# Output projection by Strassen's scheme over all sixteen row tiles, and a changed order in the last attention pair

## The reference

```python
SEQ, D_MODEL = 1024, 2048
def hybrid_layer(x, ..., w_out):
    proj = jnp.einsum('bsd,de->bse', rms_norm(x, norm_g), w_in)
    ...
    mixed = jnp.concatenate([out_a * silu(az), out_b * silu(bz), out_c * silu(cz)], axis=-1)
    return x + jnp.einsum('bse,ed->bsd', mixed, w_out)
```

## Time and profile before

| | |
|---|---|
| timed runs, median of 3 | 2040.82 us (2039.97 to 2043.32) |
| profiled execution | 2044.43 us |
| its span, first to last instruction | 2042.7 us |
| TensorE busy | 2008.2 us, 98% |
| VectorE, ScalarE, GpSimd busy | 1121.9, 891.1, 503.1 us |
| plain second column group, first matmul | 1785.5 us |
| Strassen part, first matmul | 1872.6 us |
| Strassen part, last matmul | 2037.3 us |

### The profile page before, as it was taken

The page is one execution under the profiler, slowest core; times in us unless marked ns, Lnnn a source line. Parts: engine busy times, 40 slices in busy tenths (PEclk is TensorE's granted clock), DMA queues, the critical chain, the costliest instruction groups (busy, mean ns, idle before and its releaser), DMA issues.

```text
span 2042.7 us, 28729 instructions
## 1 busy us (share of the span) xinstructions
PE 2008.2 (98%) x10024; PEld 1690.6 (83%) x10024; DVE 1121.9 (55%) x1733; ACT 891.1 (44%) x1504; POOL 503.1 (25%) x400
## 2 busy tenths in 40 slices
PE   6999999999999999999999999999999999999998
PEld 5788888888888888888888888888888887788787
DVE  7611456465445555555555555555555657613797
ACT  7311343444454445445454445445444556411242
POOL 0000343251531212222221212222122210002565
PEclk9999999999999999999999999999999999999999
DMA  7322424324332222222222222323232274466646
GB/s 236 81 72 71 116 68 109 100 82 103 94 98 78 61 85 78 87 67 72 87 72 85 64 89 79 107 58 98 83 97 71 85 249 145 134 200 222 237 155 196
DMA packets 204559, 223.20 MB, mean 109 GB/s; under 512 B 17336, under 2 KB 143336, under 8 KB 203328
## 3 DMA queue, kind: packets, MB, share of 16 engines
...
...
## 4 chain that ended last, share of the span: by engine, by line
PE 85%; DVE 7%; ACT 2%; DMA 2%; issue 2%; POOL 1%; SPq 0%; DVEq 0%; ACTq 0%; POOLq 0%
PE acc L2266 19%; PE acc L2268 19%; PE acc L2267 19%; PE pv L2504 4%; PE turned L2489 4%; PE scores L2481 2%; PE scores L2478 2%; DVE w_lo L1724 1%; DVE act_lo L2209 1%; DMA w_raw<-in_w_in_dram 1%; PE acc L2616 1%; DVE fast_out L2222 1%; PE acc L2553 1%; PE acc L2555 1%; PE acc L2554 1%
## 5 line engine op out<-in xcount | busy, mean ns | idle before, releaser
L2266 PE MATMUL acc<-act_hi,w_hi 128*128 128x512 f32 x1848 | 737.1, 399 | 2.5 <-DVE w_lo L1724 1.9
L2268 PE MATMUL acc<-act_hi,w_lo 128*128 128x512 f32 x1848 | 722.0, 391 | 0.0
L2267 PE MATMUL acc<-act_lo,w_hi 128*128 128x512 f32 x1848 | 720.7, 390 | 0.0
L2268 PEld LDWEIGHTS acc<-act_hi,w_lo 128*128 128x128 f32 x1848 | 346.9, 188 | 75.4
L2266 PEld LDWEIGHTS acc<-act_hi,w_hi 128*128 128x128 f32 x1848 | 347.5, 188 | 69.5 <-DVE w_lo L1724 4.8
L2267 PEld LDWEIGHTS acc<-act_lo,w_hi 128*128 128x128 f32 x1848 | 347.7, 188 | 65.2
L1724 DVE TENSOR_TENSOR w_lo<-w_raw,w_hi 128x512 fp32r<-128x512 f32 x223 | 199.4, 894 | 358.6 <-ACT w_hi L1239 358.3
L1545 ACT ACTIVATE prob<-prob,neg_max 128x128 f32<-128x128 f32 (+7 forms) x160 | 124.0, 775 | 251.1 <-DVE neg_max L2035 251.1
L1159 POOL TENSOR_TENSOR vz<-raw 32x512 f32<-32x512 f32 x72 | 85.6, 1189 | 468.3 <-ACT sq L1492 465.6
L1239 ACT ACTIVATE w_hi<-w_raw 128x512 fp32r<-128x512 f32 x223 | 139.1, 624 | 137.2 <-PE acc L2268 110.1
L2051 DVE TENSOR_TENSOR pt_lo<-turned,pt_hi 128x1024 fp32r<-128x1024 f32 (+1 forms) x120 | 114.9, 957 | 146.9 <-ACT pt_hi L1553 146.3
...
## 6 DMA issues: line engine op xcount, KB each, us to landing
...
```

The costliest lines, as they stand in the source:

```text
L2266: pe.matmul(acc, hi, xh, start=first, stop=False)
L2267: pe.matmul(acc, hi, xl, start=False, stop=False)
L2268: mm = pe.matmul(acc, lo, xh, start=False, stop=end)
```

## The change

The halves of row tiles now have eight tiles each, tile 8 and tile 9 among them, so that the only left run is the one item of the first column group, which stands first. There are 57 items. For this the last two rows of `mixed` are stored to DRAM, from where halves are loaded again. The products stand in another order, with other blocks. Products 2 and 6 (`FAST_ON_TOP`) start without clearing their banks and add onto what products 0 and 4 left there, after these were merged into one block; the sum goes into the other block. That saves merges: 40 and the 8 of the left run in place of 72. A run's merges are spread over 6 steps (`MERGE_STEPS`). The row sums stand at other steps, eight for each of five products. The buffers of the three output column groups change roles.

In the last pair VectorE does the sums of rounds 0 and 1 in front of the weight split that is due there, and at slot 28 (`LATE_FIRST`) the scale in front of a split.

```diff
@@ -112,31 +112,33 @@
...
 MIX_BUFS = 4
+LATE_FIRST = 28
 
...
 FAST_CGS = (2, 3)
-FAST_ROWS = (list(range(7)), [7] + list(range(LAST + 1, KT)))
-FAST_LEFT = (LAST - 1, LAST)
+FAST_ROWS = (list(range(LAST - 1)), [LAST - 1] + list(range(LAST + 1, KT)) + [LAST])
 FAST_K = len(FAST_ROWS[0])
-FAST_WEIGHTS = (((0, 1), ALU.subtract, (1, 1)), ((1, 0), ALU.subtract, (0, 0)), ((0, 0), ALU.add, (1, 1)),
-                ((0, 0), None, None), ((1, 1), None, None), ((0, 0), ALU.add, (0, 1)), ((1, 0), ALU.add, (1, 1)))
-FAST_ROW_SUMS = (None, None, ((0, 0), ALU.add, (1, 1)), ((1, 0), ALU.add, (1, 1)), ((0, 0), ALU.add, (0, 1)),
-                 ((1, 0), ALU.subtract, (0, 0)), ((0, 1), ALU.subtract, (1, 1)))
-FAST_INTO = (((1, 0, ALU.add), (1, 1, ALU.add)), ((0, 1, ALU.add), (0, 0, ALU.add)),
-             ((0, 0, ALU.add), (1, 1, ALU.add)), ((0, 1, ALU.add), (1, 1, ALU.subtract)),
-             ((1, 0, ALU.add), (0, 0, ALU.subtract)), ((1, 1, ALU.add),), ((0, 0, ALU.add),))
-FAST_RUNS = [("product", 0), ("product", 1), ("left", 0), ("left", 1), ("left", 2)] + [("product", q) for q in range(2, 7)]
-LEFT_ROWS = (FAST_LEFT, FAST_LEFT, FAST_LEFT[1:])
-LEFT_COLS = (FAST_CGS[0] * HALF, FAST_CGS[1] * HALF, 0)
+FAST_WEIGHTS = (((0, 1), ALU.subtract, (1, 1)), ((1, 0), ALU.subtract, (0, 0)), ((0, 0), ALU.add, (0, 1)),
+                ((0, 0), None, None), ((0, 0), ALU.add, (1, 1)), ((1, 1), None, None), ((1, 0), ALU.add, (1, 1)))
+FAST_ROW_SUMS = (None, None, ((1, 0), ALU.subtract, (0, 0)), ((1, 0), ALU.add, (1, 1)), ((0, 0), ALU.add, (1, 1)),
+                 ((0, 0), ALU.add, (0, 1)), ((0, 1), ALU.subtract, (1, 1)))
+FAST_ON_TOP = (2, 6)
+FAST_INTO = (((1, 0, ALU.add),), ((0, 1, ALU.add), (0, 0, ALU.add)), ((1, 1, ALU.add),),
+             ((0, 1, ALU.add), (1, 1, ALU.subtract)), ((1, 1, ALU.add),), ((1, 0, ALU.add), (0, 0, ALU.subtract)),
+             ((0, 0, ALU.add),))
+FAST_RUNS = [("left", 2)] + [("product", q) for q in range(7)]
+LEFT_ROWS = {2: (LAST,)}
+LEFT_COLS = {2: 0}
 RUN_SIZE = [FAST_K if kind == "product" else len(LEFT_ROWS[q]) for kind, q in FAST_RUNS]
...
 FAST_SLOTS = 4
+MERGE_STEPS = 6
 SPLIT_BEFORE = Q_OUT + EARLY + KT
...
 FAST_SUMS = (len(FAST_INTO) - 2) * FAST_K
-ROW_SUM_STEP = [first + j for first in (9, 16, 23, 30, 37) for j in range(FAST_K)]
+ROW_SUM_STEP = [first + j for first in (4, 12, 20, 28, 36) for j in range(FAST_K)]
 MERGES = []
@@ -241,7 +243,7 @@
...
         elif e < n:
-            out += own[2 * (n - e - 1):2 * (n - e)]
+            out += [own[i] for i in range(len(own)) if e + 1 + i * MERGE_STEPS // len(own) == n]
     return out
@@ -549,7 +551,7 @@
...
         t_los = [t_lo0[:], t_lo1[:], w_lo[:, 0, :], w_lo[:, 1, :]]
-        merged_into = [fast_out[0], fast_out[1], res]
+        merged_into = [res, fast_out[1], fast_out[0]]
 
@@ -931,8 +933,11 @@
...
                 load_early_rows(n)
+                if n == 7:
+                    store_pair(LAST - 1)
                 if n == 10:
                     sp.wait_ge(mix_lo, mixed_by(KK_GATED, 1))
+                    sp.wait_ge(mixed_saved, 16 * LAST)
                     load_gate(LAST, last_column)
@@ -959,20 +964,27 @@
...
 
-            def load_fast_residual(c, t):
-                cols = slice(FAST_CGS[c] * HALF, (FAST_CGS[c] + 1) * HALF)
-                sp.dma_start(fast_out[c][:, t, :], x_rows[t * P:(t + 1) * P, cols]).then_inc(x_in[c], 16)
+            def load_fast_residual(t):
+                cols = slice(FAST_CGS[1] * HALF, (FAST_CGS[1] + 1) * HALF)
+                sp.dma_start(fast_out[1][:, t, :], x_rows[t * P:(t + 1) * P, cols]).then_inc(x_in[1], 16)
 
             def load_partial(t):
+                sp.dma_start(fast_out[0][:, t, :], partial[t * P:(t + 1) * P, :]).then_inc(x_in[0], 16)
+
+            def load_first_residual(t):
+                cols = slice(FAST_CGS[0] * HALF, (FAST_CGS[0] + 1) * HALF)
                 sp.wait_ge(out_saved[t], 32)
-                sp.dma_start(res[:, t, :], partial[t * P:(t + 1) * P, :]).then_inc(res_in[t], 16)
+                sp.dma_start(res[:, t, :], x_rows[t * P:(t + 1) * P, cols]).then_inc(res_in[t], 16)
 
...
                 k = FAST_ROWS[kh][j]
-                sp.wait_ge(quarter_done, 3 * (GROUPS + AHEAD) + EARLY - len(ROUNDS) + OUT_ORDER.index(k) + 1)
+                if k == LAST:
+                    sp.wait_ge(out_ready, 2 * NT)
+                else:
+                    sp.wait_ge(quarter_done, 3 * (GROUPS + AHEAD) + EARLY - len(ROUNDS) + OUT_ORDER.index(k) + 1)
                 sp.dma_start(raw_rows(th, kh, j), mixed[k * P:(k + 1) * P, th * HALF:(th + 1) * HALF])\
-                    .then_inc(mix_in[0 if th == kh else 1 + kh], 16)
+                    .then_inc(mix_in[2 * kh + (th != kh)], 16)
 
@@ -999,7 +1011,10 @@
...
                 load_out_quarter(1, kk)
+            sp.wait_ge(o_done, LAST + 3)
+            sp.dma_start(mixed[LAST * P:(LAST + 1) * P, :], vz[:]).then_inc(mixed_saved, 16)
             sp.wait_ge(mix_lo, MIX_ALL)
+            sp.wait_ge(mixed_saved, 16 * PAIRS)
             load_res(1)
@@ -1013,37 +1028,40 @@
...
                         for t in range(2 * (kk - 8), 2 * (kk - 8) + 2):
-                            load_fast_residual(1, t)
+                            load_fast_residual(t)
                 else:
-                    load_rows_again(1, 1, kk - 12)
+                    if kk == 12:
+                        load_rows_again(0, 0, FAST_K - 1)
+                    load_rows_again(1, 0, kk - 12)
                     for t in range(2 * (kk - 12), 2 * (kk - 12) + 2):
-                        load_fast_residual(0, t)
+                        load_partial(t)
             load_terms(2)
-            load_rows_again(1, 1, 4)
+            load_rows_again(1, 0, 4)
             load_terms(3)
-            load_rows_again(1, 1, 5)
+            load_rows_again(1, 0, 5)
             load_terms(4)
             load_terms(5)
-            load_rows_again(1, 1, 6)
+            load_rows_again(1, 0, 6)
             load_terms(6)
             load_terms(7)
+            load_rows_again(1, 0, 7)
             for n in range(8, FAST_ITEMS):
...
                 if 8 <= n < 8 + FAST_K:
-                    load_rows_again(1, 0, n - 8)
+                    load_rows_again(1, 1, n - 8)
                 if 14 <= n < 18:
                     for t in range(2 * (n - 14), 2 * (n - 14) + 2):
-                        load_partial(t)
+                        load_first_residual(t)
                 if 18 <= n < 18 + FAST_K:
                     load_rows_again(0, 1, n - 18)
-                if 28 <= n < 32:
-                    for t in range(2 * (n - 28), 2 * (n - 28) + 2):
+                if 20 <= n < 24:
+                    for t in range(2 * (n - 20), 2 * (n - 20) + 2):
                         save_merged(2, t)
-                if 45 <= n < 49:
-                    save_merged(0, 4 + n - 45)
+                if 48 <= n < 52:
+                    save_merged(0, 4 + n - 48)
             for t in range(4):
@@ -1209,9 +1227,12 @@
...
                 if u == 0:
-                    pool.wait_ge(mix_in[0], mix_landed(0) + 16 * 2 * FAST_K)
-                elif j == 0 and q in (3, 4):
-                    pool.wait_ge(mix_in[q - 2], mix_landed(q - 2) + 16 * FAST_K)
+                    pool.wait_ge(mix_in[0], mix_landed(0) + 16 * FAST_K)
+                    pool.wait_ge(mix_in[1], mix_landed(1) + 16 * FAST_K)
+                elif j == 0 and q == 3:
+                    pool.wait_ge(mix_in[2], mix_landed(2) + 16 * FAST_K)
+                elif j == 0 and q == 5:
+                    pool.wait_ge(mix_in[3], mix_landed(3) + 16 * FAST_K)
                 if u >= 4:
@@ -2132,14 +2153,18 @@
...
                 for slot in range(8, SLOTS + 1):
-                    for n in early_at(slot):
-                        if n % (KT - 1) == 0 and n > 0:
-                            early_sums(n // (KT - 1) - 1)
                     steps(slot)
+                    if slot == LATE_FIRST:
+                        late(slot)
                     for n in early_at(slot)[:1]:
+                        if n % (KT - 1) == KT - 2 and n < EARLY - 1:
+                            early_sums(n // (KT - 1))
                         split_next(n + EARLY_AHEAD)
-                    late(slot)
+                    if slot != LATE_FIRST:
+                        late(slot)
                     for n in early_at(slot)[1:]:
+                        if n % (KT - 1) == KT - 2 and n < EARLY - 1:
+                            early_sums(n // (KT - 1))
                         split_next(n + EARLY_AHEAD)
@@ -2211,10 +2236,10 @@
...
                 r, b, c, t, op = MERGES[i]
-                if c == 2:
+                if merged_before(i) is None and c == 0:
                     dve.wait_ge(res_in[t], 48)
                 elif merged_before(i) is None:
-                    dve.wait_ge(x_in[c], 16 * (NT // X_BUFS + NT))
+                    dve.wait_ge(x_in[c % 2], 16 * (NT // X_BUFS + NT))
```

(8 more changed lines are left out.)

## The result

| | before | changed |
|---|---|---|
| timed runs, median | 2040.45 us (2039.58 to 2043.32, 16 runs) | 2044.53 us (2043.22 to 2046.54, 16 runs) |
| ratio | | 1.0020, 95% interval 1.0013 to 1.0027 |
| profiled execution | 2044.43 us | 2045.13 us |
| its span | 2042.7 us | 2043.4 us |
| Strassen part, first to last matmul | 164.71 us | 169.78 us |

The change costs 4.1 us, 0.2%. The forecast was 2043.7, in a range of 2036.5 to 2049.5.

What follows compares the result with a forecast made beforehand. TensorE's matmuls were taken as the bound, as long as VectorE and GpSimd keep up. -2.75 - 2.5 + 5.5 + 3.2 - 0.6 = +2.85 us, set on the 2040.82 median: 2043.7 us, range 2036.5 to 2049.5.

Steps and rivals of the forecast that it cites:

- 12 matmuls fewer: Strassen part: 696 matmuls in place of 708, at 0.23 us each, all on the path, -2.75 us.
- The idle time of the leftover runs: Strassen part: TensorE's waits for banks VectorE has still to merge, a weight split and refills all go, -2.5 us.
- Full clock in every slice: Whole kernel: TensorE is granted full speed in every profile slice, so clock plays no part.
- First stretch: Items 8 to 24: 17 steps with weight and row sum outrun the weights' head start, 5.5 us waiting (3.5 to 10).
- The price of a double step: A step where GpSimd has both weight and row sum takes 3.43 us, against TensorE's 2.755 an item.
- rival B: Items 8 to 24: the weights' load, sum and split loop becomes the slower bound, +7.9, 2048.7 us; chance 0.27.
- Second stretch: Items 33 to 40: eight steps with both sums cost 6.0 us, 2.8 regained before: 3.2 us waiting (2 to 5).
- Last pair: VectorE order edits: first round's sums 0, second round's +0.5, slot 28's scale -1.1; together -0.6 us (-1.2 to +0.5).
- Loads and stores: Two new 512 KB stores of mixed rows and reordered loads cost 0; +1.4 us if the cover is short.
- The signs: Strassen waits name weights' low parts, VectorE busy throughout early items, subtractions 1.3 us and over; last-pair waits 0.4, over 1.
- A: Strassen part: new waits stay away because GpSimd's sums run ahead, gain -5.85, 2035.0 us; chance 0.16.
- C: Steps with both sums: VectorE and GpSimd exclude each other wholly, 3.8 us a step, +10.4, 2051.2 us; chance 0.03.

Runs made afterwards that it cites:

- experiment 1: The kernel before, unchanged, run and profiled a second time: 2039.62 us, ratio 0.9995, profiled at 2040.18 us.
- experiment 4: Changed kernel with GpSimd's weight sums replaced by one constant write (2033.63 us), then by three writes taking nearly a sum's time (2034.42 us); one execution each.
- experiment 2: The kernel before with only the changed VectorE order of the last pair: 2039.44 us, ratio 0.9995.
- experiment 5: Changed kernel with the second column group's stores cut to 16 of 512 columns: 2043.61 us, one execution.
- experiment 6: Changed kernel with row sums of products 3 to 6 at later steps, spreading steps that have both weight and row sum: 2042.93 us, ratio 1.0011.
- experiment 8: Changed kernel with only stores moved: first column group's to items 28 to 31, last group's second half before its first: 2044.88 us, ratio 1.0027.
- experiment 3: Changed kernel with the old VectorE order in the last pair, so the Strassen part's change alone: 2043.65 us, ratio 1.0018.

## Why the prediction was right, point by point

The time came out 0.8 us above the forecast, in its mechanism. As a difference the miss is larger: +2.85 us were forecast and +4.1 measured; the three runs that the forecast was set on had a median 0.4 us above that of the sixteen, and that part of the closeness is luck. Step by step, against the profile of experiment 1:

- *12 matmuls fewer, -2.75.* Right: without a wait (experiment 4) the part takes 159.28 us, 695 x 0.2292.
- *The idle time of the leftover runs, -2.5.* It goes, but in an ordinary execution it is 1.74 us. The term was read from the profiled execution of before, and is 0.8 us too large. Nor is it all the leftover runs': in experiment 2's profile most of it stands in front of low parts.
- *Full clock in every slice.* Too coarse a reading: the slice is 51 us long and hid 3.4 us at half clock. It belonged to no edit, but I set the difference on the median without knowing why the execution was slow.
- *First stretch, +5.5 (3.5 to 10).* 5.9 to 7.2. The price of a double step (3.43) and the lead (6.7 at item 8) were right to 0.05 us; of what is missing, experiment 5 puts 0.6 to 1.9 us down to the second group's stores in full queues, which I had only in rival B.
- *Second stretch, +3.2 (2 to 5).* 3.3 to 3.6, by two errors that cancel: the lead at item 32 was 3.4 us and not 2.8, and the double steps behind it used 6.7 and not 6.0.
- *Last pair, 0, +0.5, -1.1.* +0.1, +0.45 and -1.12, each at its place.
- *Loads and stores, 0.* Right for the changed kernel, and only because double steps covered them: experiments 6 and 8.
- *The end.* Not in my sum: the last matmul to the end is 0.44 us shorter (4.36 against 4.80), and the last merge ends 1.19 us after the last matmul in place of 1.54.

- *The signs.* The waits name `t_lo` and `w_lo`, come at the items said, and those of the last pair are at 0.34 and 1.10. Two signs came only in part: the means are over 1.3 us for the row splits (1.42) but not for the weights' (1.21 for `w_lo` over the whole part), and VectorE is busy behind 1900 us but idle for 12.5 of the 20 us before, which was B's sign.

The balance, with the 0.6 us by which the Strassen part starts earlier (1869.25 against 1869.87): -2.75 - 1.74 + 10.5 - 0.44 - 0.6 = +5.0 us, and the spans are 2043.4 - 2038.4 = 5.0. With the 9.5 us of waits of experiments 3 and 8 it is +4.0, near the difference of the medians, 4.1. The 0.6 closes the balance of these two executions and is no measurement of the last pair: with its new order the starts lie from 1867.9 to 1870.9 us in eleven profiles, with the old one at 1869.5, 1869.9 and 1872.6.

Of the rivals, A is out: the waits came. C is out at 3.40 us a double step; it had added 1.29 and 0.6 as if nothing overlapped. B is partly true: from item 8 to item 12 the low parts came 15.24 us apart in the changed kernel's profile, B's round of 15.1, but behind item 12 at 3.40 us an item and not at its 3.77.
